# A transformer pair on one core: cross output product by tiles, RMS factor at the evacuations, and a denser deal of the sparse mixer's steps

## The reference

```python
# layer l of the first block
h = memory_cross_attention(x, mem, x_wq[l], x_wkv[l], x_wo[l])   # o.reshape(B, S, 512) @ wo
x = layer_norm(ALPHA * x + h, ln2_g[l], ln2_b[l])
h = conv_ffn(x, ...)
x = layer_norm(ALPHA * x + h, ln3_g[l], ln3_b[l])
# the second block, layer 0
xn = rmsnorm(h, norm_mix[0])          # xf * rsqrt(mean(xf * xf) + EPS) * g
proj = xn @ w_in                      # q, k, v, u, iq, iw, ik
s = einsum('bqhd,bsd->bqhs', iq, ik)  # 16 index heads
scores = einsum('bqhs,bqh->bqs', relu(s), iw)
_, idx = top_k(where(causal, scores, -inf), 128)
# attention of each query over its 128 picked keys only
```

## Time and profile before

| | |
|---|---|
| time, median of 3 runs (range) | 3519.42 us (3517.09 to 3521.35) |
| the profiled execution | 3520.43 us, span 3518.6 us |
| TensorE busy | 3421.1 us, 97% |
| VectorE, ScalarE, GpSimd busy | 53%, 40%, 7% |
| mean granted clock of TensorE | 0.99 |
| the chain that ended last | TensorE 85%, VectorE 8%, ScalarE 3% |

### The profile page before, as it was taken

How to read it: one execution, slowest core, us unless ns; L and a number is a source line. 1 busy time by engine, 2 the same in 40 slices (tenths; PEclk the granted TensorE clock), 3 DMA queues, 4 the chain that set the end, 5 groups by cost and what they waited for, 6 DMA issues and landing times.

```text
span 3518.6 us, 41704 instructions
## 1 busy us (share of the span) xinstructions
PE 3421.1 (97%) x16871; PEld 2856.3 (81%) x16871; DVE 1873.7 (53%) x3030; ACT 1409.1 (40%) x2497; POOL 255.4 (7%) x321
## 2 busy tenths in 40 slices
PE   9999999999999999999998989999999998999999
PEld 8888888888888888888887767888888876888887
DVE  5554566636555545666354685553333695543332
ACT  4543333424245433334243554544232565543231
POOL 1300200000031011000001020100000000100000
PEclk9999999999999999999999998999999999999999
DMA  4112241332231123322322222313223202313222
GB/s 158 60 51 79 100 155 60 102 102 96 85 114 59 44 90 132 108 84 96 102 96 65 73 76 72 130 58 98 97 98 99 84 25 93 126 54 102 96 96 78
DMA packets 89617, 316.18 MB, mean 90 GB/s; under 512 B 10704, under 2 KB 11472, under 8 KB 88912
## 3 DMA queue, kind: packets, MB, share of 16 engines
q1 hardware_dynamic: 89424, 313.51, 26.9%
HBM read 309.27 MB, written 4.19 MB: 89 GB/s over the span
## 4 chain that ended last, share of the span: by engine, by line
PE 85%; DVE 8%; ACT 3%; POOL 2%; issue 1%; DMA 0%; SPq 0%; DVEq 0%; ACTq 0%
PE bk L1088 75%; PE bk L1182 3%; PE bk L1146 2%; DVE ar L2103 2%; PE bk L1156 1%; PE bk L1102 1%; PE bk L1231 1%; POOL st L2184 1%; DVE wl L1693 1%; POOL x L2252 1%; POOL st L2186 1%; DVE x L1722 1%; DVE xl L1706 0%; DMA wr<-in_wpk 0%; DVE st L1806 0%
## 5 line engine op out<-in xcount | busy, mean ns | idle before, releaser
L1088 PE MATMUL bk<-xh,wh 128*128 128x512 f32 (+1 forms) x2216 | 838.4, 378 | 8.3 <-DVE xl L1706 8.3
L1088 PE MATMUL bk<-xh,wl 128*128 128x512 f32 (+1 forms) x2216 | 830.8, 375 | 0.0
L1088 PE MATMUL bk<-xl,wh 128*128 128x512 f32 (+1 forms) x2216 | 830.1, 375 | 0.0
L1693 DVE TENSOR_TENSOR wl<-wr,wh 128x1024 fp32r<-128x1024 f32 (+1 forms) x372 | 450.5, 1219 | 676.3 <-ACT wh L1344 674.8
L1344 ACT ACTIVATE wh<-wr 128x1024 fp32r<-128x1024 f32 (+1 forms) x372 | 386.7, 1047 | 736.6 <-PE bk L1088 685.1
L1088 PEld LDWEIGHTS bk<-xh,wh 128*128 128x128 f32 x2216 | 418.8, 189 | 81.5 <-issue 9.5
L1088 PEld LDWEIGHTS bk<-xh,wl 128*128 128x128 f32 x2216 | 418.5, 189 | 75.8
L1088 PEld LDWEIGHTS bk<-xl,wh 128*128 128x128 f32 x2216 | 418.9, 189 | 71.9
L1088 PE MATMUL bk<-wh,ah 128*128 128x512 f32 x1184 | 465.4, 393 | 5.8 <-DVE al L2148 3.9
L1088 PE MATMUL bk<-wh,al 128*128 128x512 f32 x1184 | 461.8, 390 | 0.0
L1088 PE MATMUL bk<-wl,ah 128*128 128x512 f32 x1184 | 461.6, 390 | 0.0
(11 more groups left out here) (279 smaller groups left out, 4110.0 us busy)
## 6 DMA issues: line engine op xcount, KB each, us to landing
wr<-in_wpk SPq DMA_DIRECT2D x540, 512.0 KB, 3.3
gb<-in_ln_g SPq DMA_DIRECT2D x6, 512.0 KB, 4.2
gb<-in_ln_b SPq DMA_DIRECT2D x6, 512.0 KB, 5.4
ar<-in_xT SPq DMA_DIRECT2D x8, 256.0 KB, 6.5
wr<-in_wpk SPq DMA_DIRECT2D x8, 256.0 KB, 6.0
ar<-in_memT SPq DMA_DIRECT2D x2, 1024.0 KB, 4.9
x<-in_x SPq DMA_DIRECT2D x4, 512.0 KB, 5.3
park<-x SPq DMA_DIRECT2D x4, 512.0 KB, 6.1
```

The source lines that it names most:

```text
L1088: i = pe.e.matmul(dst, lw, rw, start=g not in opened, stop=end)
L1693: dve.e.tensor_tensor(m.wl[:, s, a], m.wr[:, r, a], m.wh[:, s, a].bitcast(F32), ALU.subtract) \
```

## The change

The cross attention of the first block no longer calls `residual` but `by_tiles`, which computes both halves of a row tile before it goes to the next. Stage 5 (the FFN ahead of the sparse mixer) no longer scales its rows by the RMS factor before they are transposed: it transposes the layer norm's output, and the evacuations of the mixer's products multiply by the factor. A product waits for the part of a tile's `xl` that it reads and not for the second one. In the sparse mixer the deal per product step is three steps of `side` instead of two from the first transposed index queries to the last scores, and seven picks instead of three once q and k are both transposed.

```diff
--- before.py
+++ after.py
@@ -346,6 +346,34 @@
                     self.rest = [("turn", si, 1)] + late + [("turn", si, 3)]
             yield from self.gemm(G, None, tail=tail)
 
+    def by_tiles(self, si, name, idx, nk, op):
+
+        halves = [Gemm(si, "res", (hf, True, True), nk, ((name, idx, hf * 512, hf * 512 + 512),), op, "T", 4)
+                  for hf in range(2)]
+        self.last_res = halves[1]
+        for t in range(NT):
+            for G in halves:
+                G.grp.append(self.take())
+            for u in range(halves[0].nu):
+                for G in halves:
+                    ks = G.ks(u)
+                    if t == 0:
+                        G.unit[u] = self.use((ks[0], len(ks), G.pieces, None))
+                    self.add("mm", G, u, [t], None, t == NT - 1)
+                    if t == NT - 1:
+                        self.rel += 1
+                        self.prefetch(G.unit[u])
+                if t == 0 and u == 0:
+                    while self.held:
+                        self.held.pop(0)()
+            self.add("ev", halves[0], t)
+            self.give(halves[0].grp[t])
+            if t < 2:
+                self.close(si, t)
+            elif t == 2:
+                self.turn_x(si, 0)
+        self.rest = [("turn", si, 1), ("norm", si, 2), ("norm", si, 3), ("turn", si, 2), ("turn", si, 3)]
+
 
     def attend(self, A, put, hold=False):
 
@@ -540,7 +568,7 @@
         drive((self.gemm(G, self.ev(G)), 1))
         A = Att(("X", l), si, 4, 128, 256, lambda t: (0, 2))
         drive((self.attend(A, self.put(A), True), 1))
-        drive((self.residual(si, "x_wo", l, 4, "att"), 1))
+        self.by_tiles(si, "x_wo", l, 4, "att")
 
     def ffn(self, si, l):
         one = si < 6
@@ -683,7 +711,10 @@
                          lambda: part("iq", 1, 2560, 3072, count=n_iq), project)
         side = chain(keys, lambda: queries(0), lambda: scores(0), lambda: queries(1), lambda: scores(1), turns)
         chooser, pool = choose(), pools()
-        beside(products, (side, 2), (chooser, 3), (pool, 1))
+        for _ in products:
+            for steps, n in ((side, 3 if 0 in turned and len(scored) < NT else 2), (chooser, 7 if len(pro) == 2 else 3), (pool, 1)):
+                for _ in range(n):
+                    next(steps, None)
         beside(side, (chooser, 2))
         A = Att(("M", 0), si, 4, 128, 512, lambda t: (0, t + 1))
 
@@ -967,6 +998,10 @@
     def slot(self, si, t):
         return self.u(12288 + 1024 * (t % 2), 1024) if si == 5 else self.gb[:, t % 2, :]
 
+    def rs(self, t):
+
+        return self.st[:, 244 + t:245 + t]
+
     def crms(self, j, t):
         a = 66 + 2 * (4 * j + t)
         return self.st[:, a:a + 2]
@@ -1049,7 +1084,7 @@
                         pe.wait_ge(*ev["xt", k])
                     else:
                         for t in tiles:
-                            pe.wait_ge(*ev["xs", G.si, t])
+                            pe.wait_ge(*ev["xs", G.si, t, k // 4 * 4])
                 elif G.op == "mg":
                     pe.wait_ge(*ev["merged", G.si, k])
                 elif G.op == "mem":
@@ -1096,8 +1131,8 @@
     def turn_x(si, t, j, g):
         ps = begin(g)
         pe.wait_ge(*ev["d_cst"])
-        src = m.slot(si, t) if si >= 5 else m.x[:, t, :]
-        pe.wait_ge(*ev["xn" if si >= 5 else "ln", si, t])
+        src = m.slot(si, t) if si >= 6 else m.x[:, t, :]
+        pe.wait_ge(*ev["xn" if si >= 6 else "ln", si, t])
         for q in range(4):
             i = pe.e.transpose(ps[:, tile(q)], src[:, tile(j + q)], ident)
         i.then_inc(*ev.up("pe_at", ("grp", g), ("turned", si, t, j)))
@@ -1360,10 +1395,12 @@
             act.wait_ge(*ev["ln", si, t])
         else:
             act.wait_ge(*ev["res", si, 1, t])
-        if t >= 2:
+        if t >= 2 and si > 5:
             act.wait_ge(*ev["turned", si, t - 2, 4])
         act.e.activation(m.slot(si, t), m.x[:, t, :], ACT.Square, bias=0.0, scale=1.0, accum_out=ss) \
             .then_inc(*ev.up("act_ev", ("ss", si, t)))
+        if si == 5:
+            return
         act.wait_ge(*ev["ss", si, t])
         act.wait_ge(*ev["rs", si, t])
         act.e.activation(m.slot(si, t), m.x[:, t, :], ACT.Copy, scale=rs).then_inc(*ev.up("act_ev", ("xn", si, t)))
@@ -1517,17 +1554,18 @@
                 act.wait_ge(*ev["prod", G.si, f])
                 act.e.activation(m.ah[:, f % 12, :], b, ACT.Copy).then_inc(*ev.up("x_hi", ("hid_hi", G.si, f)))
         elif G.kind == "iq":
-            act.e.activation(m.iqs[G.tag][:, o, :], psum(g)[:, :], ACT.Copy) \
+            act.wait_ge(*ev["rs", 5, o])
+            act.e.activation(m.iqs[G.tag][:, o, :], psum(g)[:, :], ACT.Copy, scale=m.rs(o)) \
                 .then_inc(*ev.up("act_ev", done, ("iq", G.tag, o)))
         elif G.kind == "ik":
             act.e.activation(m.ikr, psum(g)[0:80, :], ACT.Copy).then_inc(*ev.up("act_ev", done, "ik"))
         elif G.kind == "mq":
-            act.e.activation(m.mraws[G.tag][:, o, :], psum(g)[:, :], ACT.Copy) \
+            act.e.activation(m.mraws[G.tag][:, o, :], psum(g)[:, :], ACT.Copy, scale=m.rs(o)) \
                 .then_inc(*ev.up("act_ev", done, ("mq", G.tag, o)))
         elif G.kind in ("mv", "mu"):
             dst = m.mvt[:, o, :] if G.kind == "mv" else m.mut[:, o, :]
             act.wait_ge(*ev["causal", 3])
-            act.e.activation(dst, psum(g)[:, :], ACT.Copy).then_inc(*ev.up("act_ev", done, (G.kind, o)))
+            act.e.activation(dst, psum(g)[:, :], ACT.Copy, scale=m.rs(o)).then_inc(*ev.up("act_ev", done, (G.kind, o)))
         elif G.kind == "cin" and o < 2:
             m0 = G.tag
             ps = psum(g)
@@ -1704,7 +1742,7 @@
         ps = bk[sc.bank[g]]
         dve.wait_ge(*ev["xs_hi", si, t, j])
         dve.e.tensor_tensor(m.xl[:, j:j + 4, tile(t)], four(ps), m.xh[:, j:j + 4, tile(t)].bitcast(F32), ALU.subtract) \
-            .then_inc(*ev.up("x_lo", ("free", g), *([("xs", si + 1, t)] if j == 4 else [])))
+            .then_inc(*ev.up("x_lo", ("free", g), ("xs", si + 1, t, j)))
 
     def ln(si, t):
         x, st = m.x[:, t, :], m.st[:, t * 16:t * 16 + 12]
@@ -2019,8 +2057,11 @@
 
     def ik_back(g):
         ps = four(psum(g))
-        dve.e.tensor_scalar(m.iw, ps[:, :, 0:16], 1.0 / 32.0, None, ALU.mult)
-        dve.e.tensor_copy(m.ik, ps[:, :, 16:80]).then_inc(*ev.up("dve_ev", ("free", g)))
+        for t in range(NT):
+            dve.wait_ge(*ev["rs", 5, t])
+        rs = lambda n: m.st[:, 244:248].unsqueeze(2).broadcast_to([128, NT, n])
+        dve.e.scalar_tensor_tensor(m.iw, ps[:, :, 0:16], 1.0 / 32.0, rs(16), ALU.mult, ALU.mult)
+        dve.e.tensor_tensor(m.ik, ps[:, :, 16:80], rs(64), ALU.mult).then_inc(*ev.up("dve_ev", ("free", g)))
         cos, sin = (m.c(n).rearrange("p (t f) -> p t f", t=NT) for n in ("cosi", "sini"))
         x1, x2 = m.ik[:, :, 0:8], m.ik[:, :, 8:16]
         q = [m.itmp[:, a * 32:a * 32 + 32].rearrange("p (t f) -> p t f", t=NT) for a in range(4)]
@@ -2353,7 +2394,7 @@
             sp.e.dma_start(m.x[:, t, :], src[tile(t), :]).then_inc(*ev.up(f"d_back{t}", ("d_back", l, t), by=16))
 
     def m2_loads():
-        sp.wait_ge(*ev["xs", 6, 3])
+        sp.wait_ge(*ev["xs", 6, 3, 4])
         sp.e.dma_start(m.mgain[0], row("a_q_norm_2", 0, 128)).then_inc(*ev.up("d_gain0", ("d_gain", ("M", 0), 0), by=16))
         sp.e.dma_start(m.mgain[1], row("a_k_norm_2", 0, 128)).then_inc(*ev.up("d_gain1", ("d_gain", ("M", 0), 1), by=16))
 
```

## The result

The changed kernel takes **3489.45 us** (median of 4 runs, 3488.14 to 3490.97), the kernel before 3518.39 (4 runs), a ratio of 0.9917 with the interval 0.99 to 0.9934. The forecast was 3490.7. The profiled execution took 3490.97 us, the longest of the four, with a span of 3489.2.

A forecast was written before the change was run, and what follows sets the result against it. TensorE, busy 3421.1 of 3518.6 us, was taken as the bound, leaving its gaps and lower-clock time to win. Terms 3.9 + 11.4 + 1.9 + 11.5 = 28.7 us; 3519.4 - 28.7 = 3490.7 us, range 3479 to 3504, chance 0.50.

The forecast's parts named there:

- Cross product: Two cross output products with the FFN's start: computing by tiles removes early waits, new wait at tile 3's transposes; 3.9 us for both.
- The lower bound: Two cross output products: -1 us, if the new wait at tile 3's transposes costs the clock again.
- RMS factor: Stage 5 into the sparse mixer: scaled copies and roots leave the path to the transposes; 11.4 us, bounds 8 and 13.
- First `xl` part: Three more stage starts: TensorE waits for one part instead of two, 0.64 us each; 1.9 us, bounds 0 to 3.
- Deal: Sparse mixer: 12 picks move from beside the attention into VectorE's earlier waits; 11.5 us, bounds 0 and 20.
- (1): Mixer and FFN starts: VectorE gets no nearer, deal gives 3 us, cross products 1, rest 13; 3502 us; chance 0.17.
- (2): All three stretches: the clock comes back too, deal gives 18 us, cross products 7; 3481 us; chance 0.17.
- (3): Mixer: GpSimd's eight multiplications each hold a VectorE instruction, item 0 comes 4 us later; 3495 us; chance 0.10.
- (4): Mixer steps 17 to 19: splits queue behind 21 picks, TensorE waits; 3523 us or slower, 3528; chance 0.05.

## Why the prediction was right

The forecast (3490.7) and its sum (28.7 us) held; the measured difference is 28.9 us. Three additions in it are off by 0.1 us: 1.2, 1.4 and 0.64 make 3.2 and not 3.1, the cross part adds up to 3.8 and not 3.9, and 15.9 - 2.9 - 2.4 + 1 is 11.6. Step by step:

**Cross product.** The mechanism was as told: the first FFN product 2 us sooner (2.9, or 2.2 counted from the product's end), one new wait of 2.3 us at tile 3's transposes (2.5). Wrong was that no wait for VectorE stays at tile 1: the transposes' second part takes a bank that tile 3's first sum frees, and the working had followed the input and not the bank, 1.27 us. The lower bound said that the new wait might cost the clock again. It does in some executions: in both layers of the profiled one, which is why its own trace shows at most 1.5 us for a term of 3.9. Taking the part back cost 2.9 to 3.9 us.

**RMS factor.** Two waits of 1.1 and 1.5 us were forecast, of 1.08 and 1.27 found; clock 1.00 as told. Between the two profiled executions the step is worth 12.1 us (13.55 in front of the mixer less the 1.48 already won), by taking it back 9.7 to 10.7. The lower figure is for the most part the clock of the old way, which fell less in that trace than in the one of before: 0.96 over the 84.3 us of its way into the mixer, against 0.94 over 85.8 before, with TensorE busy for 73.8 us instead of 75.5 for the same 329 matmuls.

**First `xl` part.** Three starts of 0.64 us: the waits went from 1.66, 1.66 and 1.67 us to 1.07 each. That there are more places was not in the term: the mixer's own start, which hides in the late RMS factor's gain, and a stage start at 955 us with three waits of 0.2 us.

**Deal.** 11.5 us forecast, 11.5 between the profiled executions (offset 13.55 ahead of it, 25.09 behind), 10.2 to 11.2 by taking it back. Inside the sum three entries were off against each other: item 0 came 1.2 us later against its stage (2104.71 less 2092.40 is 12.3, of 13.5; 2.9 forecast), the seven items took 9.8 us (9), and the 1 us of half clock saved behind them did not come: from item 7 to the stage's end it is 28.5 us in both traces. The stage's products ended 2.3 us later against theirs, since TensorE waits 4.6 us at the q and k transposes where it waited 3.1; the sum has no such entry and needs none, for TensorE then waits for item 0 in any case. About 10 us of waits were to stay, 5 for the scores and 3.5 for the first rotary embedding; 4.6 and 3.7 did, with 0.9 elsewhere.

**Something not forecast** also moved: between 2800 and 2930 us the changed kernel gained 2.2 us in the convolution module's statistics, which the change doesn't touch. The clock was 0.54 in the worst 10 us there before and 0.69 after, and the other kernels gained anything from 0 to 2.4 us at this place. It stood in for what the cross part lacked in this execution: 1.5 for the cross part, 12.1, 1.8 and 11.5 for the others and these 2.2 us are 29.1 of the 29.4 us between the two profiled spans. So a part of the exact hit is luck.

**The rivals.** VectorE did get nearer (1). The clock came back halfway, 0.88 instead of 0.75, so (2) gave none of its extra 9 us. Of (3), collisions with GpSimd, the number stayed at four, but they moved. Before, one instruction each was held by about 1 us in the norms (1.70 us for two), the rotary subtraction (1.20), a split (2.45 for two) and another rotary step (1.33). Now the longest split and the longest score are ordinary. Held are the rotary subtraction three times, by 1.0 us, and the mask over tile 1's scores, 1.25 us where it took 0.29. The groups (ns min/median/max), then two collisions, a subtraction and the mask on VectorE and the multiplications on GpSimd beside them, which take 1.29 us otherwise; last the three masks before:

```profile
L1737 DVE SCALAR_TENSOR_TENSOR wl<-wr,par,wh x31: 740/745/762, 1929.6 to 2058.0; 128x512 fp32r<-128x512 f32 x31
...
L2046 DVE TENSOR_TENSOR ar<-ar x16: 224/226/1209, 1941.3 to 2048.2; 128x64 f32<-128x64 f32 x16
...
2015.63 1.21 DVE L2046 TENSOR_TENSOR ar<-ar 128x64 f32<-128x64 f32 x1
...
2015.23 1.52 POOL L2310 TENSOR_TENSOR ar<-ar 128x512 f32<-128x512 f32 x1
...
2034.49 1.25 DVE L2109 TENSOR_SCALAR ar<-ar 128x256 f32<-128x256 f32 x1
...
2034.30 1.29 POOL L2310 TENSOR_TENSOR ar<-ar 128x512 f32<-128x512 f32 x1
...
L2068 DVE TENSOR_SCALAR ar<-ar x3: 294/359/427, 2060.7 to 2126.9; 128x256 f32<-128x256 f32 x1, 128x384 f32<-128x384 f32 x1, 128x512 f32<-128x512 f32 x1
```

That VectorE and GpSimd hold each other is what the Trainium skill's page "SBUF — State Buffer", section "Who interferes with whom", says, and these rows agree. The mask reads only one operand from SBUF, so the case of two inputs that the prediction names is not the only one that is held. Applied without the places, the rule gave (3) eight held instructions, four more than before. The scores had ended by 2004.8 us, ahead of the first multiplication at 2008.55, and the splits fell between the multiplications, one with an overlap of 0.2 us. (4) is real, but its price comes from the q and k chain and not from splits.

## What to carry to other kernels

Work that fills an engine's waits must be there when the wait comes, and work moved ahead of a meeting point pays only where it finds such a wait: opening the source of the picks earlier brought 2.7 us, dealing more of them 4.6, and only both the whole 10.2. Before an order is made denser, look for what has no look-ahead behind it in the same queue: that, not the prefetched splits, stopped TensorE for 30 us. And where a second engine sets the next meeting point, a gap or a low clock ahead of it is free and one behind it costs in full, so a gap total of the same size can be a different time: 4.6 us of idle time stand in a cross stretch of 45.2 us at a clock of 0.96, and in one of 43.7 us at 1.00 (with products that wait for both `xl` parts).

## What the runs showed of the hardware

The same program with the same waits takes 3488.1 to 3491.5 us, in two groups some 2 us apart; nine runs are few for calling them two levels. In the cross stretch the difference is visible in the rows: the granted clock was 0.83 either in 580 to 590 us or in 590 to 600, and only the second lengthened the stretch, by 1.5 us. A mask of VectorE over 128x256 scores in SBUF took 1.25 us beside a multiplication on GpSimd and 0.29 without one, as a subtraction of two 128x64 operands took 1.21 and 0.22. I had not expected that one profiled execution may be off by 2 to 3 us for such a part, as much as the part is worth.
